# Counted unused products in TensorE's waits at fourteen places, and the low parts of two output matrices moved from GpSimd to VectorE

## The reference

```python
def second_block(x, positions, ...):
    for layer in range(2):
        h = rmsnorm(x, attn_norm[layer])
        if layer == 0:
            x = x + even_mixer(h, even_w_in, sinks, rel_bias_table, even_w_out)
        else:
            x = x + mla_mixer(h, positions, ..., mla_w_o)
        h = rmsnorm(x, ffn_norm[layer])
        x = x + swiglu(h, ffn_w_gate[layer], ffn_w_up[layer], ffn_w_down[layer])
    return rmsnorm(x, final_norm)

# even_mixer: proj = h @ w_in; o_a = stick_breaking(q_a, k_a, v_a)
#             o_b = sliding_window(q_b, k_b, v_b); return concat(o_a, o_b) @ w_out
# mla_mixer:  16 heads, softmax of (q_nope.k_nope + q_rope.k_rope) * scale; return out @ w_o
```

## Time and profile before

| | |
|---|---|
| median of 3 runs | 1426.02 us (1424.97 to 1426.74) |
| the profiled execution: its time, its span | 1425.24 us, 1423.4 us |
| PE busy | 1346.5 us, 95% of the span |
| DVE, ACT, POOL busy | 899.2, 641.7, 281.6 us |
| chain that ended last | PE 86%, DVE 7%, ACT 3%, DMA 1% |
| mean granted TensorE clock | 0.962 of full speed |
| HBM | 187 MB, 132 GB/s over the span |

### The profile page before, as it was taken

The page is one execution under the profiler, slowest core; times in us unless marked ns, Lnnn a source line. Parts: engine busy times, 40 slices in busy tenths (PEclk is TensorE's granted clock), DMA queues, the critical chain, the costliest instruction groups (busy, mean ns, idle before and its releaser), DMA issues.

```text
span 1423.4 us, 27091 instructions
## 1 busy us (share of the span) xinstructions
PE 1346.5 (95%) x10342; PEld 1173.9 (82%) x10342; DVE 899.2 (63%) x1750; ACT 641.7 (45%) x1240; POOL 281.6 (20%) x341
## 2 busy tenths in 40 slices
PE   7999999899899989999998989899999999899998
PEld 6898888789778888999987955588888886788886
DVE  5666666645658876778846444667654765577654
ACT  4344444433134434676635334544343576443433
POOL 0002322212334340223301021111210122022200
PEclk9999999999799989999998968999999999899999
DMA  7312111024312125455555420255555451255452
GB/s 298 120 63 87 62 61 61 32 64 148 146 63 75 72 75 185 156 177 180 191 189 183 165 85 31 89 178 185 198 181 203 148 178 60 90 184 200 179 204 90
DMA packets 26774, 189.90 MB, mean 133 GB/s; under 512 B 2960, under 2 KB 3088, under 8 KB 4400
## 3 DMA queue, kind: packets, MB, share of 16 engines
q1 hardware_dynamic: 25632, 182.51, 35.9%
q0 software_dynamic: 1040, 5.96, 1.4%
HBM read 186.37 MB, written 1.05 MB: 132 GB/s over the span
## 4 chain that ended last, share of the span: by engine, by line
PE 86%; DVE 7%; ACT 3%; DVEq 1%; issue 1%; DMA 1%; POOL 0%; POOLq 0%; ACTq 0%; SPq 0%
PE ps L569 33%; PE ps L517 13%; PE ps L597 11%; PE ps L599 6%; PE ps L832 5%; PE ps L679 1%; PE ps L668 1%; PE ps L851 1%; PE ps L1073 1%; PE ps L549 1%; PE ps L542 1%; PE ps L486 1%; PE ps L541 1%; PE ps L797 1%; PE ps L931 1%
## 5 line engine op out<-in xcount | busy, mean ns | idle before, releaser
L1369 ACT ACTIVATE w_hi<-ring 128x1024 fp32r<-128x1024 f32 x125 | 132.6, 1061 | 319.0 <-PE ps L569 177.8
L597 PE MATMUL ps<-h_both,w_hi 128*128 128x512 f32 x704 | 246.8, 394 | 2.0 <-DVE h_both L1867 2.0
L1897 DVE TENSOR_TENSOR w_lo<-ring,w_hi 128x1024 fp32r<-128x1024 f32 x117 | 145.4, 1243 | 136.1 <-ACT w_hi L1369 135.9
L599 PE MATMUL ps<-h_both,w_lo 128*128 128x256 f32 x704 | 198.1, 281 | 0.0
L569 PE MATMUL ps<-h_both,w_hi 128*128 128x256 f32 x1008 | 185.6, 287 | 2.3 <-DVE h_both L1867 2.3
L569 PEld LDWEIGHTS ps<-h_both,w_hi 128*128 128x128 f32 x1008 | 160.4, 196 | 3.3 <-issue 3.3
L597 PEld LDWEIGHTS ps<-h_both,w_hi 128*128 128x128 f32 x704 | 132.8, 189 | 32.1 <-issue 2.6
L1903 DVE TENSOR_TENSOR w_lo<-ring,w_hi 128x1024 fp32r<-128x1024 f32 x117 | 147.4, 1260 | 0.0
L517 PE MATMUL ps<-oT_r,ring_r 128*128 128x256 f32 x512 | 146.3, 286 | 0.0
L569 PE MATMUL ps<-h_both,w_lo 128*128 128x256 f32 x504 | 144.3, 286 | 0.0
L599 PEld LDWEIGHTS ps<-h_both,w_lo 128*128 128x128 f32 x704 | 134.2, 191 | 0.0
(11 more groups left out here) (411 smaller groups left out, 2946.2 us busy)
## 6 DMA issues: line engine op xcount, KB each, us to landing
ring<-in_weights SPq DMA_DIRECT2D x170, 1024.0 KB, 4.8
arena<-in_aux POOLq DMA_DIRECT2D x1, 2112.0 KB, 12.8
grow<-in_rows POOLq DMA_DIRECT2D x3, 512.0 KB, 4.4
cst<-in_consts SPq DMA_DIRECT2D x1, 1497.5 KB, 15.1
x<-in_x SPq DMA_DIRECT2D x1, 1024.0 KB, 4.9
arena<-in_swbias POOLq DMA_DIRECT2D x1, 1024.0 KB, 7.1
arena<-arena POOLq DMA_DIRECT2D x1, 1024.0 KB, 9.0
out<-xn SPq DMA_DIRECT2D x4, 256.0 KB, 2.3
```

The lines of the kernel that those rows point to most:

```text
L597: pe.matmul(bank[:].rearrange("p (a t) -> p a t", a=2), hi, h_both[:, :, k, :], start=k == 0, stop=False)
L599: m = pe.matmul(bank[:, 0:S], lo, h_hi[:, k, :], start=False, stop=k == KT - 1)
L1369: act.activation(w_hi[:, half_of(u0, m), WH:], ring[:, (u0 + m) % RING, WH:], ACT.Copy).then_inc(w_hi_p, 1)
L1897: dve.tensor_tensor(w_lo[:, half_of(u0, m), WH:], ring[:, (u0 + m) % RING, WH:], w_hi[:, half_of(u0, m), WH:].bitcast(F32), ALU.subtract). ...
```

## The change

1. **Unused products.** A new helper, `idle_products(n, bank)`, issues n products of 128 x 128 by 512 columns on rounded numbers that happen to lie in a tile, into a bank that nobody reads; they wait for nothing and nobody waits for them. They stand in `normed(r)` ahead of the first wait (18, 18, 9, 6 and 11) and behind the transposes (5 each), ahead of the GELU wait (9), at the end of three phases (7, 5 and 3), behind the first group's dense pieces (5), ahead of the rows of the NSA heads (10), in the even heads' rounds 0 to 5 (2 each, 18 in round 2) and in round 2 of the MLA heads (9). That is 163 in all.
2. **Low parts.** POOL's `split_whole` goes. DVE gets `out_weights`: both halves of units 0 and 1 at the end of its rounds 1 and 2 (MLA: 4 and 5), one half each at the end of rounds 11 and 12, 15 and 16.
3. **High parts.** ACT's `out_weights` moves from the head to the end of its round, and the units 2 and 3 are split one half a round (10 and 11, 14 and 15).
4. **Banks.** `post_norm` holds its fourth piece in bank 0 in place of bank 3, behind one more drain, so that bank 3 is free for the unused products.

The diff, cut to its core, in the order PE, ACT, DVE, POOL:

```diff
+            def idle_products(n, bank, rows=oT_r):
+                for _ in range(n):
+                    pe.matmul(bank[:], rows[:, 0, 0:P], flat(rows[:])[:, 0:512], start=True, stop=True)
...
             def normed(r):
+                idle_products((18, 18, 9, 6, 11)[r], ps[3])
                 for b in range(NB):
...
+                idle_products(5, ps[7])
...
             m.then_inc(unit_done, 1)
+            idle_products(9, ps[7])
             pe.wait_ge(hid_ready, 1)
...
-            phase_end(pe)
+            phase_over(pe)
+            idle_products(7, ps[7])
+            pe.wait_ge(phase, 4 * phases[id(pe)])
...
+                if g == 0:
+                    idle_products(5, ps[7])
                 pe.wait_ge(c_exp, g + 1)
...
+            idle_products(10, ps[0])
             pe.wait_ge(gb_done, 8)
             transposes(o_rows)
...
+            def even_idle(s):
+                if s < 6:
+                    idle_products(18 if s == 2 else 2, ps[6])
+            def mla_idle(s):
+                if s == 2:
+                    pe.wait_ge(kv_out, 5)
+                    idle_products(9, ps[3])
...
             for s in range(H + 3):
-                out_weights(U["even_out"], s)
...
+                out_weights(U["even_out"], s)
...
+            def out_weights(u0, name, s, s0=0):
+                if s in (s0 + 1, s0 + 2):
+                    split_unit(u0, name, s - s0 - 1)
+                if s in (11, 15):
+                    first_half(u0, name, s // 4)
+                if s in (12, 16):
+                    second_half(u0, name, s // 4 - 1)
...
-            for m in range(4):
-                split_whole(U["even_out"], "even_out", m)
```

More of the change, by code:

```diff
@@ L649, in out_rows, with heads_pipeline @@
                 pe.drain().then_inc(unit_done, 1)
-            def heads_pipeline(t0, scores, bank_free, p_ready_of, values, fill, early=iter(())):
+            def heads_pipeline(t0, scores, bank_free, p_ready_of, values, fill, idle, early=iter(())):
                 for s in range(H + 3):
@@ L660, in heads_pipeline @@
                         next(early, None)
+                    idle(s)
                     if s >= 6:
@@ L1098, in _ @@
                 pass
+            idle_products(10, ps[0])
             pe.wait_ge(gb_done, 8)
             transposes(o_rows)
-            phase_end(pe)
+            phase_over(pe)
+            idle_products(5, ps[0], hT_r)
+            pe.wait_ge(phase, 4 * phases[id(pe)])
             late = ONE + 8
@@ L1156, in _ @@
                 m.then_inc(unit_done, 1)
-            phase_end(pe)
+            phase_over(pe)
+            idle_products(3, ps[6])
+            pe.wait_ge(phase, 4 * phases[id(pe)])
             def even_scores(s, bank):
@@ L1185, in even_values @@
                 return vb[:, kt, (s - SB_HEADS) // 4 * HD:((s - SB_HEADS) // 4 + 1) * HD]
-            heads_pipeline(0, even_scores, even_bank_free, even_p, even_values, out_rows("even_out", 0))
+            def even_idle(s):
[5 more added lines that the diff above has]
+                    idle_products(9, ps[3])
+            heads_pipeline(0, even_scores, even_bank_free, even_p, even_values, out_rows("even_out", 0),
+                           even_idle)
             normed(2)
@@ L1280, in _ @@
                            lambda h: pe.wait_ge(a_p, SW_HEADS + h + 1), mla_values, out_rows("mla_out", KT),
-                           late_units())
+                           mla_idle, late_units())
             normed(4)
@@ L1363, in split_rows_of_heads, with high_p @@
                     act.activation(flat(hi)[:, q * 512:(q + 1) * 512], ps[4 + q][:], ACT.Copy).then_inc(h_hi_ready, 1)
-            def split_unit(u0, m, i=0):
+            def high_p(u0, m, i=0):
                 arrived(act, u0 + m, i)
@@ L1370, in split_unit, with high_d @@
                                ACT.Copy).then_inc(w_hi_p, 1)
+            def high_d(u0, m, i=0):
                 act.activation(w_hi[:, half_of(u0, m), 0:WH], ring[:, (u0 + m) % RING, 0:WH],
                                ACT.Copy).then_inc(w_hi_d, 1)
+            def split_unit(u0, m, i=0):
+                high_p(u0, m, i)
+                high_d(u0, m, i)
             def softmax_exp(t, j, sink=None):
@@ L1399, in out_weights @@
                 if s in (s0, s0 + 1):
-                    if s == s0:
-                        act.wait_ge(unit_done, u0)
+                    act.wait_ge(unit_done, u0)
                     split_unit(u0, s - s0)
-                if s in (9, 13):
-                    m = (s - 1) // 4
-                    act.wait_ge(unit_done, u0 + m - 1)
-                    split_unit(u0, m)
+                if s in (10, 14):
+                    act.wait_ge(unit_done, u0 + s // 4 - 1)
+                    high_p(u0, s // 4)
+                if s in (11, 15):
+                    high_d(u0, s // 4)
             def ffn_units(u0, body, tail=None):
@@ L1770, in _ @@
             for s in range(H + 3):
-                out_weights(U["mla_out"], s, 3)
                 if s < H:
@@ L1780, in _ @@
                     out_high(KT + (s - 4) // 2)
+                out_weights(U["mla_out"], s, 3)
             boundary(4, U["up2"], small("g_ffn2")[:, KT:2 * KT])
@@ L1831, in gained @@
                     dve.wait_ge(post_sq, 4 * n_post + q + 1)
-                    dve.tensor_tensor(ps[q][:], ps[4 + q][:], grow[:, (q % 2) * 512:(q % 2 + 1) * 512], ALU.mult)
+                    dve.tensor_tensor(ps[q % 3][:], ps[4 + q][:], grow[:, (q % 2) * 512:(q % 2 + 1) * 512], ALU.mult)
                 dve.wait_ge(row_in, 16 * (n_post + 1))
@@ L1838, in post_norm @@
                     if b == 1:
+                        dve.drain()
                         gained(3)
@@ L2407, in _ @@
                     out_low((s - 4) // 2)
+                out_weights(U["even_out"], "even_out", s)
             first_half(U["up1"], "ffn1", 0)
@@ L2512, in _ @@
                     out_low(KT + (s - 4) // 2)
+                out_weights(U["mla_out"], "mla_out", s, 3)
             first_half(U["up2"], "ffn2", 0)
@@ L2563, in root_x @@
                                        ALU.pow).then_inc(row_rstd, 1)
-            def split_whole(u0, name, m):
-                pool.wait_ge(w_hi_p, SPLIT[name] + m + 1)
-                pool.sem_inc(apart, 1)
-                pool.tensor_tensor(w_lo[:, half_of(u0, m), WH:], ring[:, (u0 + m) % RING, WH:],
-                                   w_hi[:, half_of(u0, m), WH:].bitcast(F32), ALU.subtract).then_inc(w_lo_p, 1)
-                pool.wait_ge(w_hi_d, SPLIT[name] + m + 1)
-                pool.sem_inc(apart, 1)
-                pool.tensor_tensor(w_lo[:, half_of(u0, m), 0:WH], ring[:, (u0 + m) % RING, 0:WH],
-                                   w_hi[:, half_of(u0, m), 0:WH].bitcast(F32), ALU.subtract).then_inc(w_lo_d, 1)
             def split_one(m):
@@ L2707, in _ @@
             pool.dma_start(kmT[HD:P], kr[HD:P].unsqueeze(1).broadcast_to((HD, H, S))).then_inc(kr_all, 16)
-            for m in range(4):
-                split_whole(U["mla_out"], "mla_out", m)
             root_x(4)
```

3 lines of the change are left out of this document (2 added, 1 removed).

## The result

The changed kernel took 1402.26 us (median of 4 runs, 1399.68 to 1404.58), the kernel before 1426.38 us beside it (1424.97 to 1427.93): ratio 0.9826, 95% interval 0.9803 to 0.9849, 24.1 us faster. The forecast was 1395.8 us, in a range of 1384 to 1409: the direction and the main causes were right, the gain was 6.5 us too large.

A forecast was written before the change was run, and what follows sets the result against it. PE bounds the kernel, with 99.1 us in eight half-clock stretches. Gains 8.4 + 2.5 + 2.4 + 11.2 + 6.2 less 0.3 and 0.2 make 30.2 us: 1425.24 to 1395.0, median 1395.8 us, range 1384 to 1409.

The forecast's parts named there:

- The product's price: One unused product of 512 columns costs 0.227 us of PE at full clock, 0.45 us at half, nothing inside a wait.
- what the clock answers to: At all places of unused products: the granted clock counts products nobody reads; full speed gives back at most 50 us.
- the rival "slower": All fourteen places: the clock does not answer to unused products, which run at half clock; 37 us added, 1454 us; 3%.
- the rival of the boundaries that stay low: Five boundaries: the clock falls again during the 16 transposes, so their gain stays away; 1406.6 us; chance 7%.
- The boundaries: Five boundaries r = 0 to 4: full clock gains 8.4 us together, at least 3, at most 15.
- The two drains: Two more drains in `post_norm`: a cost of 0.2 us, from an estimate of 0.1 each, bounds 0 and 1.
- The compressed branch: NSA groups, stretch of 17.1 us: at full clock PE goes from sums to next scores faster; gain 2.5 us, bounds 0 and 8.5.
- The NSA branch's end: Transposes of the heads' rows and some 14 products leave half clock; gain 2.4 us, bounds 0 and 5.
- The even heads: Up to head 7's scores: full clock and moved low parts together gain 11.2 us, bounds 3 and 17.
- The contended rounds: Four sliding-window rounds, two in even heads, two in MLA, fall from 5.10 to 3.56 us: gain 6.2 us, bounds -3.7 and 7.
- the rival of DVE as the bound: In the heads, DVE's added halves make it the bound; up to 9.9 us lost in late rounds, 1405.7 us; chance 12%.
- The first rounds of MLA: POOL's hold on DVE goes, but nine products and crowded parts cost PE; loss 0.3 us, bounds -3 and +3.

## Why the prediction came out as it did

**The product's price** (0.227 us) and **what the clock answers to**: right. Products that nobody reads keep the granted clock; the rival "slower" is out, and so is the rival of the boundaries that stay low. At r = 0 the 16 transposes ran at 1.00 behind the 18 products, 1.06 and 1.09 us for eight each (timeline):

```profile
569.37 1.06 PE L492 MATMUL ps<-cst,xn 128*128 128x128 f32 x8 [0.30 <-DVE xn L1897]
...
570.98 1.09 PE L492 MATMUL ps<-cst,xn 128*128 128x128 f32 x8 [0.55 <-DVE xn L1900]
```

By the rule that the Trainium skill gives ("TensorE: Matmul & The Clock Gate", Part 4: PE-mode transpose), that full clock does not engage for transposes, this stretch would have been slow; the trace does not bear it out.

**The boundaries**, 8.4 us: measured 7.6, each within 0.2 us but r = 1 (2.1 in place of 2.7). The sizes fit the trace they were read from, but that trace does not stand for every execution: the second trace of the kernel before lost only some 0.9 us of r = 4's 3.2 and nothing at r = 3. Some 4 us of the 8 that I read off one trace depend on the execution. The five products behind the transposes cost nothing that shows at r = 2, as taken. The two drains, entered at an estimate of 0.2 us that no row gave, cost 0.18 us each, also in the version with no product; the three products at the last phase cost another 0.18.

**The compressed branch**, 2.5 us of gain forecast: the step that failed, 1.0 us lost in the trace, 3.5 us off. I had seen that POOL holds DVE there and charged it up to 385.39 only; I took group 1's pace at full clock for what follows, although there DVE's two low halves were hidden by PE's slow products. At full clock they are late next, and the waits brought the clock down in groups that had been fast.

**The NSA branch's end**, 2.4 us: measured 2.45.

**The even heads**, 11.2 us: measured 10.7, from the phase's start to head 7's scores 25.8 us, where 26 was forecast; sliding-window rounds took 3.56 and 3.57 us, one of them 3.80. The number is right, in part by luck; the reading that all these products earn it is wrong. I had DVE's first result and the 18 products in the same line, saw that the products and not DVE set the time, and did not draw that they were then a cost. The runs show that the moved low parts give 3.5 us with no product at all, that 12 products do more than 28 (11.3 and 12.9 us), and that with none of them in the heads, but the others in place, it is 10.6 us.

**The contended rounds**, 6.2 us: measured 8.1, because there are three such places in the even heads (1.9, 1.6 and 1.5 us) and not two. The halves on DVE cost nothing: the version without products gained the same 8.1 us, so the rival of DVE as the bound is out for these rounds.

**The first rounds of MLA**, a loss of 0.3 us: measured 3.0. The nine products were entered at their full 2.0 us, but set off against the end of DVE's hold; the runs give 2.1 us for them and 1.35 for the low stretch behind, which the prediction did not have and which stands in half of the traces with the nine. This is the second term that failed, 2.7 us off, half of it chance of the execution.

**The rest.** 2.2 us in the third FFN are a pace of the execution, and 1.0 us less at the start is too; together they do not speak for or against the change. Of the 7 us between forecast and trace, 3.5 are the compressed branch, 2.7 the MLA heads, 1.2 these two, 1.6 small terms (boundaries, even heads, drains), against 1.9 more in the contended rounds. That the sum came as near as it did is in part luck: errors of both signs, and shares of some 2 us that come and go with the execution.

## What to carry to other kernels

Unused products keep the granted clock, but only those that lie in a wait are free: read the wait again in the kernel in which the other edits have been made, since one edit may take away the wait that another fills. Before counting what a faster TensorE (PE) brings, look for the next operation that starts with a phase or another engine and not with PE; behind it the gain turns into a wait, and the wait may take the clock with it. Take a second trace of the unchanged kernel before pricing terms of one or two us, and more than one of a version before charging a low stretch to one of its edits.

## What the runs showed of the hardware

- Dense products have two paces at full granted clock. Of 14 traces (two of them of the kernel before), the second FFN ran in 7 and the third in 11 at some 353 ns for a pair of products (512 and 256 columns), in the others at some 347 ns, with the same code: 2.1 to 2.3 us an FFN. No run told what sets it.
- Whether and for how long the clock falls behind a wait differs between executions and between versions with the same code at that place: r = 3 and r = 4 in the two traces of the kernel before; r = 2 in the two versions without products at the boundaries, and not in the two traces of the kernel before; 3.4, 6.8 or 10.2 us in the NSA groups; 3.4 us or nothing in the MLA projections (nine of fourteen traces) and in the first MLA heads (three of six with the nine). What decides it was not found.
- GpSimd holds some of DVE's operations for as long as one of its instructions lasts: 3.87 us for 8 numbers a row beside one subtraction of 4.56 us, 0.60 us when it was cut in four. The operations held ended when GpSimd's did (383.08 and 383.06 us). Two DVE operations of 0.28 us just before it were not held. In four pieces GpSimd took 6.01 us, and DVE's two low halves 4.50 us in place of 2.35.
